# Expert rows weighted and gated on their way out of PSUM and added by DMA into a plane that starts as the residual

## The reference, cut to what matters

```python
x = x + g1 * mix                                        # the residual, x2 in the kernel
h = rms_norm(x, norm2_w) * (1.0 + sc2) + sh2
x = x + g2 * hier_moe(h, ...)
# hier_moe: each token takes the best of 4 groups, then the best two of its 8 experts (32 in all)
wts = p_grp * top_p / jnp.sum(top_p, axis=-1, keepdims=True)      # one weight for each of the two
hid = silu(h @ w_exp_gate[e]) * (h @ w_exp_up[e])                 # 1024 -> 256
y   = sum over the two experts of wts * (hid @ w_exp_down[e])     # 256 -> 1024
```

## Time and profile before

| | |
|---|---|
| median of three runs | 1171.54 us |
| the profiled execution's own time | 1173.27 us |
| its span, first to last instruction | 1171.5 us |
| busy: PE, DVE, ACT, POOL | 1029.5, 433.0, 311.7, 164.0 us |
| mean granted TensorE clock | 0.954 of full speed |
| moved by DMA over the span | 204.20 MB, 174 GB/s |

### The profile page before, as it was taken

One profiled execution on the slowest core, in us unless ns is written; L12 is line 12 of the kernel. 1 busy time (PEld: TensorE's weight loads), 2 busy tenths in 40 slices (PEclk: granted clock), 3 DMA queues, 4 the chain that ended last, 5 costly groups with the idle time before them and its releaser, 6 DMA issues.

```text
span 1171.5 us, 14600 instructions
## 1 busy us (share of the span) xinstructions
PE 1029.5 (88%) x5595; PEld 562.0 (48%) x5595; DVE 433.0 (37%) x845; ACT 311.7 (27%) x619; POOL 164.0 (14%) x257
## 2 busy tenths in 40 slices
PE   4999999999998889989999999999919997797870
PEld 2444456666554679988544444444513332232220
DVE  1433036787775864645501200224460111100116
ACT  4122144566652434324310000111211111111111
POOL 0100020011000327770300000000110121101110
PEclk9999999999999999999999999999959999988995
DMA  9821152436110111300371110142535999999956
GB/s 387 346 90 46 70 183 88 190 116 216 73 72 16 42 39 41 98 8 1 109 284 72 72 72 10 63 166 85 216 103 192 396 401 422 422 424 423 423 226 269
DMA packets 43644, 204.20 MB, mean 174 GB/s; under 512 B 16736, under 2 KB 22320, under 8 KB 31536
## 3 DMA queue, kind: packets, MB, share of 16 engines
q1 hardware_dynamic: 32576, 171.92, 37.3%
q0 software_dynamic: 10416, 30.45, 7.3%
q10 hardware_dynamic: 576, 0.82, 0.2%
HBM read 191.79 MB, written 19.76 MB: 181 GB/s over the span
## 4 chain that ended last, share of the span: by engine, by line
PE 75%; DVE 11%; issue 5%; DMA 5%; ACT 2%; POOL 2%; SPq 0%; POOLq 0%; DVEq 0%; ACTq 0%
PE bank L1717 25%; PE bank L2311 11%; PE bank L1839 7%; PE bank L2332 5%; PE bank L2156 3%; PE bank L2154 3%; PE bank L1681 2%; PE bank L1998 2%; PE bank L1888 2%; DMA arena<-in_w_up 2%; PE bank L2299 1%; PE bank L2008 1%; PE bank L1732 1%; DMA arena<-in_w_blocks 1%; PE bank L1824 1%
## 5 line engine op out<-in xcount | busy, mean ns | idle before, releaser
L1717 PE MATMUL bank<-arena 128*128 128x512 f32 x672 | 292.6, 591 | 0.0
L1717 PEld LDWEIGHTS bank<-arena 128*128 128x128 f32 x672 | 125.4, 189 | 151.8 <-issue 151.8
L2311 PE MATMUL bank<-arena 128*32 128x512 f32 x1152 | 140.5, 642 | 32.1 <-issue 30.8
L1839 PE MATMUL bank<-arena 128*128 128x320 f32 x384 | 120.0, 454 | 0.0
L2311 PEld LDWEIGHTS bank<-arena 128*32 128x32 f32 x1152 | 42.4, 117 | 117.9 <-issue 117.9
L1839 PEld LDWEIGHTS bank<-arena 128*128 128x128 f32 x384 | 69.7, 192 | 35.7 <-issue 11.2
L1649 DVE TENSOR_TENSOR arena<-arena,bank 128x256 f32<-128x256 f32 x18 | 7.6, 421 | 174.6 <-ACT arena L1104 174.6
L1493 DVE TENSOR_TENSOR arena<-arena,bank 128x512 f32<-128x512 f32 x10 | 6.9, 688 | 168.1 <-PE bank L2156 168.1
L2332 PE MATMUL bank<-arena 128*32 128x512 f32 x576 | 65.8, 595 | 1.0 <-DVE arena L1642 1.0
L1026 ACT ACTIVATE arena<-bank 128x512 f32<-128x512 f32 x20 | 12.0, 598 | 145.7 <-PE bank L1717 145.7
L1104 ACT ACTIVATE arena<-bank 128x256 f32<-128x256 f32 x18 | 6.9, 385 | 164.2 <-PE bank L2311 164.2
(11 more groups left out here) (315 smaller groups left out, 1387.7 us busy)
## 6 DMA issues: line engine op xcount, KB each, us to landing
arena<-in_w_up SPq DMA_DIRECT2D x32, 2048.0 KB, 18.1
arena<-in_w_blocks SPq DMA_DIRECT2D x27, 2048.0 KB, 8.0
arena<-in_w_down SPq DMA_DIRECT2D x32, 1024.0 KB, 21.9
arena<-y_scratch SPq DMA_DIRECT2D x10, 512.0 KB, 7.3
arena<-in_bias POOLq DMA_DIRECT2D x3, 1536.0 KB, 10.7
arena<-mod_scratch POOLq DMA_DIRECT2D x8, 512.0 KB, 10.9
arena<-in_x SPq DMA_DIRECT2D x5, 512.0 KB, 7.0
gram_scratch<-arena SPq DMA_DIRECT2D x10, 256.0 KB, 2.5
```

What stands on the lines that cost most here:

```text
L1717: last = mm(bank, hT[:, k, tok0[i]:tok0[i] + P], w[:, k, :], start=(k == 0), stop=(k == KC - 1))
L1839: last = mm(banks[5 + half][:, 0:HTOK], w[:, k, :], hT[:, k, half * HTOK:(half + 1) * HTOK], start=(k == 0), stop=(k == KC - 1))
L2311: last = mm(banks[2 + e % 2][at, :], rowsT[e % 2][:, k, at], eup[expert % SLOTS_W][:, k, :], start=(k == 0), stop=(k == KC - 1))
```

## The change

Weights and gate rows are put together per slot while the tiles run, the product leaves PSUM already weighted and gated, and the scatter adds it to a plane that was filled with x2. The plane is then copied to the output.

- `y_scratch` has 640 rows and 128 spare ones. SP fills it with x2 in six DMAs right after `up_in(3)`, before it waits for the route.
- The weight of a pair (fp32) is cut into three fp16 pieces, spread into `named_w`, and brought to the slots by ten more small matmuls at the head of PE's branch; five DVE instructions put the pieces together as `slot_w0` (context tokens) and `slot_w1` (latent ones).
- Per tile ACT makes context gate row x `slot_w0` (`gate_part`), DVE adds latent gate row x `slot_w1` (`gate_rest`), and both banks are multiplied with that by DVE (`out_rows`). ACT's copy of bank 6 is gone.
- An empty slot of partition p is sent to spare row 640 + p instead of being passed over. Each tile's scatter becomes two, one for each run of the tile's first expert and the rest (64 and 64 rows in twelve tiles, 96 and 32, 64 and 64 or 32 and 96 in the six wide ones), so that no token appears twice in one. Each adds to what stands in HBM, and each waits until the one before it has landed (`scattered`).
[...]
- The read-back, the weighting, gating and residual add at the end are gone. Five DMAs copy the plane from HBM to the output in HBM.

The diff, cut to its core (left out: semaphore names, places of the tables, and the branch that is not taken):

```diff
@@ -320,9 +324,14 @@
...
         rows_out = [flat(hT)[:, (2 + n) * D:(3 + n) * D] for n in range(3)]
-        slot_f = flat(merged)[:, 4 * D:4 * D + 2 * TILES]
-        empty = flat(merged)[:, 4 * D + 2 * TILES:4 * D + 4 * TILES]
-        slots = flat(merged)[:, 4 * D + 4 * TILES:4 * D + 6 * TILES].bitcast(I32).rearrange("p (n e) -> p n e", n=2)
+        per_tile = [flat(merged)[:, 4 * D + n * TILES:4 * D + (n + 1) * TILES] for n in range(14)]
+        slot_f, empty, slots, slots_to, slot_w0, slot_w1 = per_tile[:6]
+        slots, slots_to = slots.bitcast(I32), slots_to.bitcast(I32)
+        slot_p = flat(merged)[:, 4 * D + 6 * TILES:4 * D + 9 * TILES].rearrange("p (n e) -> p n e", n=3)
+        slots_moved = {64: per_tile[12].bitcast(I32), 96: per_tile[13][:, 0:6].bitcast(I32), 32: per_tile[13][:, 6:12].bitcast(I32)}
+        left = per_tile[9][:, 0:2 * T].unsqueeze(2)
+        pieces = flat(merged)[:, 4 * D + 10 * TILES:4 * D + 10 * TILES + 3 * T].bitcast(FP16).rearrange("p (a n) -> p a n", n=3)
+        gated = [x2[:, n, :] for n in range(2)]
...
+
+        def expert_rows(n):
+
+            first = next(at.start for at, q in tile_parts(n) if q != tile_parts(n)[0][1])
+            return slice(0, first), slice(first, P)
 
...
@@ -563,6 +568,9 @@
...
             up_in(3)
+            for i in range(T):
+                sp.dma_start(t["y_scratch"][i * P:(i + 1) * P, :], x2[:, i, :]).then_inc(S["y_base"], 16)
+            sp.dma_start(t["y_scratch"][TOK:TOK + P, :], x2[:, 0, :]).then_inc(S["y_base"], 16)
...
                     up_in(e)
...
+                for i in range(T):
+                    sp.wait_ge(S["y_ready"], i + 1)
+                    sp.dma_start(t["y"][i], x2[:, i, :]).then_inc(S["y_out"], 16)
             with sp.Else():
                 sp.wait_ge(S["route_ready"], 2)
+                for at, table in slots_moved.items():
+                    sp.dma_start(table[0:P - at, :], slots_to[at:P, 0:table.shape[1]]).then_inc(S["moved"], 16)
...
 
-                for n in range(3):
-                    sp.wait_ge(S[f"expert_out{n}"], 16 * len(range(n, TILES, 3)))
+                sp.wait_ge(S["scattered"], 32 * TILES)
                 for i in range(T):
-                    for r in range(2):
-                        sp.dma_start(y_part(i, r), t["y_scratch"][(r * T + i) * P:(r * T + i + 1) * P, :]).then_inc(y_loaded(i)[0], 16)
-            for i in range(T):
-                sp.wait_ge(S["y_ready"], i + 1)
-                sp.dma_start(t["y"][i], x2[:, i, :]).then_inc(S["y_out"], 16)
+                    sp.dma_start(t["y"][i], t["y_scratch"][i * P:(i + 1) * P, :]).then_inc(S["y_out"], 16)
...
@@ -731,21 +739,27 @@
...
-                pool.wait_ge(S["slots_ready"], 1)
+                pool.wait_ge(S["chosen"], 3)
+                pool.wait_ge(S["y_base"], 16 * (T + 1))
                 for e in range(TILES + 3):
+                    if e == 3:
+                        pool.wait_ge(S["moved"], 16 * 3)
                     if e < TILES:
                         if e >= 4:
                             pool.wait_ge(S["rowsT_mm"], 2 * (e - 3))
                         pool.indirect_dma_start(out=rows_in[e % 4], out_offset=None, in_=t["h_scratch"],
-                                                in_offset=bass.IndirectOffsetOnAxis(ap=slots[:, 0, e:e + 1], axis=0),
+                                                in_offset=bass.IndirectOffsetOnAxis(ap=slots[:, e:e + 1], axis=0),
                                                 bounds_check=TOK - 1, oob_is_err=False).then_inc(S[f"rows_in{e % 4}"], 16)
                     if e >= 3:
                         o = e - 3
                         pool.wait_ge(S["acc_done"], o + 1)
                         pool.wait_ge(S["s_out2"], o + 1)
-                        pool.indirect_dma_start(out=t["y_scratch"], out_offset=bass.IndirectOffsetOnAxis(ap=slots[:, 1, o:o + 1], axis=0),
-                                                in_=rows_out[o % 3], in_offset=None,
-                                                bounds_check=2 * TOK - 1, oob_is_err=False).then_inc(S[f"expert_out{o % 3}"], 16)
+                        for n, at in enumerate(expert_rows(o)):
+                            if o or n:
+                                pool.wait_ge(S["scattered"], 16 * (2 * o + n))
+                            pool.indirect_dma_start(out=t["y_scratch"], out_offset=bass.IndirectOffsetOnAxis(ap=(slots_moved[at.start] if n else slots_to)[0:at.stop - at.start, o:o + 1], axis=0),
+                                                    in_=rows_out[o % 3][at, :], in_offset=None, bounds_check=TOK + P - 1, oob_is_err=True,
+                                                    compute_op=ALU.add).then_inc(S["scattered"], 16)
...
@@ -1090,11 +1105,13 @@
...
-                def out_rows(e):
-                    act.wait_ge(S["down_mm"], e + 1)
-                    if e >= 3:
-                        act.wait_ge(S[f"expert_out{e % 3}"], 16 * (e // 3))
-                    step(sc.activation(rows_out[e % 3][:, 0:HALF], banks[6][:, :], ACT.Copy), "acc_done")
+                def gate_part(e):
+                    if e == 0:
+                        act.wait_ge(S["slot_w"], 1)
+                        act.wait_ge(S["y_base"], 16 * (T + 1))
+                    if e >= 2:
+                        act.wait_ge(S["s_out2"], e - 1)
+                    step(sc.activation(gated[e % 2], gate2_bc[:, 0, :], ACT.Copy, scale=slot_w0[:, e:e + 1]), "gated")
 
                 rowsT_out(0)
                 for e in range(TILES):
@@ -1104,17 +1121,9 @@
                     step(sc.activation(sg[:, e % 2, 0:D_FF], banks[2 + e % 2][:, 0:D_FF], ACT.Silu), "silu_done")
                     if e + 1 < TILES:
                         rowsT_out(e + 1)
-                    if 1 <= e < TILES - 1:
-                        out_rows(e - 1)
                     act.wait_ge(S["hidT_mm"], e + 1)
                     step(sc.activation(hidT[:, e % 2, 0:2 * P], banks[4 + e % 2][:, 0:2 * P], ACT.Copy), "hidT_ready")
-                out_rows(TILES - 2)
-                out_rows(TILES - 1)
-                act.wait_ge(S["weights_ready"], 1)
-                for i in range(T):
-                    act.wait_ge(*y_loaded(i))
-                    a = y_part(i, 0)
-                    step(sc.activation(a, a, ACT.Copy, scale=wts[:, 1, i, :]), "weighted")
+                    gate_part(e)
...
@@ -1569,31 +1578,39 @@
...
-            for n in range(2):
-                step(v.tensor_tensor(named[:, :, n, :], reached[:, :, 0:TILES], payload[:, :, n:n + 1].to_broadcast([P, 2 * T, TILES]), ALU.mult),
-                     "dest_ready" if n else "dve_step")
+            step(v.tensor_tensor(named, reached[:, :, 0:TILES], payload[:, :, 0:1].to_broadcast([P, 2 * T, TILES]), ALU.mult), "chosen")
...
             dve.wait_ge(S["logit_mm"], 6)
-            table = banks[0][:, 256:256 + 2 * TILES]
+            table = banks[0][:, 256:256 + TILES]
             step(v.tensor_scalar(empty, table, 0.0, float(NOWHERE), ALU.is_equal, ALU.mult))
             step(v.scalar_tensor_tensor(slot_f, table, -1.0, empty, ALU.add, ALU.add))
-            step(v.tensor_copy(slots, slot_f.rearrange("p (n e) -> p n e", n=2)), "slots_ready")
+            step(v.tensor_copy(slots, slot_f), "chosen")
             barrier(dve, 3)
+            dve.wait_ge(S["router_exp"], 1)
+            step(v.tensor_reduce(wts[:, 0], ex[:, 1, :, 0:4], AX_X, ALU.add))
+            step(v.scalar_tensor_tensor(wts[:, 0], ex[:, 1, :, 4:5], 1.0, wts[:, 0], ALU.add, ALU.mult))
+            step(v.reciprocal(wts[:, 1], wts[:, 0]))
+            step(v.tensor_tensor(wts[:, 2], wts[:, 1], ex[:, 1, :, 4:5], ALU.mult))
+            weight = wts[:, 1:3].rearrange("p r t n -> p (r t) n")
+            step(v.tensor_copy(pieces[:, :, 0:1], weight))
+            step(v.tensor_tensor(left, weight, pieces[:, :, 0:1], ALU.subtract))
+            step(v.tensor_scalar(pieces[:, :, 1:2], left, float(PIECE), None, ALU.mult))
+            step(v.scalar_tensor_tensor(left, pieces[:, :, 1:2], -1.0 / PIECE, left, ALU.mult, ALU.add))
+            step(v.tensor_scalar(pieces[:, :, 2:3], left, float(PIECE * PIECE), None, ALU.mult))
+            step(v.tensor_tensor(named_w, reached[:, :, 0:TILES].unsqueeze(2).to_broadcast([P, 2 * T, 3, TILES]),
+                                 pieces.unsqueeze(3).to_broadcast([P, 2 * T, 3, TILES]), ALU.mult), "chosen")
+            step(v.tensor_scalar(slot_f, slot_f, payload[:, 0, 1:2], None, ALU.min))
+            step(v.tensor_copy(slots_to, slot_f))
             one = [1, N_RANKED, N_RANKED]
...
             step(v.tensor_reduce(order_f[0:1].unsqueeze(2), holds, AX_X, ALU.add))
             step(v.tensor_copy(order[0:1], order_f[0:1]), "route_ready")
-            dve.wait_ge(S["router_exp"], 1)
-            step(v.tensor_reduce(wts[:, 0], ex[:, 1, :, 0:4], AX_X, ALU.add))
-            step(v.scalar_tensor_tensor(wts[:, 0], ex[:, 1, :, 4:5], 1.0, wts[:, 0], ALU.add, ALU.mult))
```

(44 more changed lines are left out.)

35 lines of the change are left out of this document (17 added, 18 removed).

## The result

The changed kernel takes 1231.87 us, the median of five runs (1220.24 to 1236.13), the kernel before 1172.03 (five runs, 1170.84 to 1175.04). The ratio is 1.0493, 95% interval 1.0467 to 1.0518: 5% slower. 1195 was predicted, 1162 to 1228 the range. The direction was right; the size was not, and the measured median lies 4 us above the range.

What follows compares the result with a forecast made beforehand. From tile 9 PE waits for weights on full DMA engines. First scatter at 902.2, eight pairs at 15, eight at 19.1, 12.2 for the last two, then 0.2 and a 7.8 copy gave 1195.2 us; range 1162 to 1228.

Steps and rivals of the forecast that it cites:

- Forecast A: Tile stage: the chain of scatters paces the tiles, 1195 us, own range 1183 to 1215, chance 0.42.
- The signs named for it: Trace: paired scatters waiting on scatters, up matmuls 18 us apart or more from tile 9, DMA share below 0.98.
- B: DMA engines: chain hides behind weights, only bytes cost; with the adding's read paid 1176 to 1187 us, chance 0.18.
- C: DMA engines, 900 to 1122 us: adding costs only its writes, 9.4 us against 15.5 gained; 1165 us, chance 0.20.
- E: Whole kernel: gain and bytes cancel within 2.3 us, or the end isn't shorter; 1173 us, chance 0.05.
- eight early pairs: First eight tiles' scatter pairs: 15 us each, between PE's own pace of 12.0 and 19.1 where engines are full.
- eight pairs under load: Next eight tiles, engines full: 19.1 us per scatter pair, two landings of 9.4 us with 0.3 us of issue.
- last two pairs: Tiles 16 and 17, emptying queues: 6.1 us per scatter pair, two landings of 2.9 us and 0.3.
- hand-over and copy: After the last scatter: 0.2 us, then 7.8 us for copying 2.62 MB HBM to HBM.
- with 0.3 us of issue: Price of a tile's two chained scatters: 0.3 us of issue besides two landings, 19.1 us where engines are full.
- D: Tile stage: adding slower than thought, 19.1 us a tile or more from the first tile; 1228 up to 1240, chance 0.15.
- The end: After the last tiles: copy replaces read-back and DVE work, 15.5 us gained, 7.6 at the least, if load is gone.

Runs made afterwards that it cites:

- e4: Kernel before with each tile's scatter in two halves, each waiting for the last landing; plain writes, live rows only, old end: 1195.57 us.
- e9: Kernel before with each scatter in two plain halves and no wait between them, live rows only, old end: 1174.37 us.
- e10: e3 with a wait for the previous landing before each whole-tile adding scatter: 1175.67 us.
- e3: Changed kernel with one whole adding scatter per tile, no waits between scatters, each pair in its own row, empty slots passed over: 1173.16 us.
- e7: Kernel before plus the six DMAs filling the plane with the residual, and the waits for them: 1172.59 us.
- e8: Changed kernel's weighting and gating out of PSUM, but one plain unchained scatter per tile, no filling, read-back and DVE adds at the end: 1168.53 us.
- e1: Changed kernel with scatters writing instead of adding; split, chain of waits and spare rows stay: 1189.44 us.
- e2: Changed kernel with empty slots passed over instead of added to spare rows; adding, split and chain stay: 1207.12 us.
- e6: Changed kernel with POOL issuing each gather ahead of the scatter of the tile five places before, not three: 1219.88 us.

## Why the prediction was right and wrong

**The bound was read rightly.** Forecast A, that the chain of scatters paces the tiles, is what the trace shows, and e4, e9 and e10 show it to be the cause. The signs named for it came: pairs whose waits end with the scatter before, up matmuls further apart (19.5 us on average from tile 9 on, 16.4 before), a DMA share below 0.98 from tile 9 on (0.97, from 1012 to 1161 us), a lower granted clock that is not on the path, DVE work gone from the end. The share is a weak sign, though: it was 0.98 from 900 to 1012 us, where the chain already set the pace. One did not come: the time after the last matmul was to be 17.5 us and is 34. B and C are out, as they had the chain hidden. What they would have been was run for the live rows only: e3 comes to 1173.2, what the change adds to its stage cost 15 us, and the end gave them back, which is the balance that E had described.

**What I priced at nothing cost nothing:** the filling (e7), the work on the engines per tile (e8: last scatter 0.7 us later than before), the tables (first scatter 1.7 us earlier than before). The split and its index columns, which had no term, cost nothing either (e9, plain).

**The sum, term by term**, against the profiled span of 1218.4 (predicted 1195.2, so 23.2 to find):

| term | predicted | measured | difference |
|---|---|---|---|
| first scatter | 902.2 | 900.5 | -1.7 |
| eight early pairs | 8 x 15 = 120 | 140.7 (17.6 each) | +20.7 |
| eight pairs under load | 8 x 19.1 = 152.8 | 144.7 | -8.1 |
| last two pairs | 2 x 6.1 = 12.2 | 21.0 | +8.8 |
| hand-over and copy | 8.0 | 11.5 | +3.5 |

**The step that failed** is "with 0.3 us of issue" in the price of a pair. The start of the next scatter comes 0.8 us after the landing that it waits for, after the first half and after the second, so a pair has 1.6 us of it and not 0.3. If every pair of the sum is read as two landings and 0.3 us, as its terms for load and for empty queues are built, the miss falls apart like this:

| | predicted | measured | difference |
|---|---|---|---|
| first scatter | 902.2 | 900.5 | -1.7 |
| 36 landings | 279.6 | 278.0 | -1.6 |
| between them | 18 x 0.3 = 5.4 | 35 x 0.81 = 28.4 | +23.0 |
| hand-over and copy | 8.0 | 11.5 | +3.5 |

The gap could have been read before: DVE's last copy ends at 1138.61 + 0.69 = 1139.30 and the scatter that it releases starts at 1140.14, 0.84 us later.

That the landings sum to what was predicted is luck, for their errors cancel. The early pair of 15 us leaves 7.4 us for a landing, and it was 8.0 on average; the loaded one took 9.4, and it was 9.2 over tiles 8 to 12 but 8.2 over the eight tiles that the sum counts; the last four took 2.9, and it was 4.7.

**The early pair** of 15 us was put between PE's 12.0 and the full load's 19.1 on the thought that emptier queues would bring the landing down. It measured 17.6, and half of the difference is the gap. The queues were not empty: the DMA share is 0.99 from 900 to 1041 us, and it was 0.99 in the same place before, where the whole scatters of the first eight tiles took nearly as long as the later ones:

```profile
L746 POOL DMA_INDIRECT y_scratch<-arena x8: 1004/1016/1027, 902.2 to 987.7; - x8
...
DMA to landing us min/median/max: 6.9/9.6/11.8
```

D had the loaded pair from the first tile on, 1228; it came nearer than A, and I had given it 0.15. But D's 19.1 is more than the early 17.6, and its end is as short as A's, so its time is near in part because two errors cancel.

**The end.** Its landings were priced with the plain 2.9 us; that an adding half takes 4.7 was in no row, but I had added something for the read under load and nothing here. The copy took 11.5 us instead of 7.8. From the start of the last multiply to the end it is 33.9 us, as long as the old end (32.9); the gain of 15.5 us that the sum counted was lost to four landings in a row. Without the chain it is there: 15.7 us in e3.

**The loaded pair** (19.1 predicted; 20.1 over tiles 8 to 13, less in the last ones) was right in size. Its landing of 9.4 us under full load was right too (9.2), but partly for a wrong reason, as the number of live rows hardly counts: over tiles 8 to 12 halves of 64 and of some 35 written rows both take 7.9 us (e1, e4). The adding counts, 9.2 us for 64 rows. On empty queues halves take 3.2 (64 written), 4.7 (64 added) and 2.5 us (35 written).

**What stays open.** The median lies 11.6 us above the profiled execution, so that much of the miss can't be read in a trace. The changed kernel spreads 16 us over five runs and e1_plain 11 over four, but e2, e4 and e6, which are chained too, only 5 over four each, so the chain alone does not explain the spread. Why landings under load differ so little with their rows (7.9 us for 35 as for 64) no run tells.

## What to carry to other kernels

A wait for a DMA's landing costs what a landing costs under the load of its stage, not on empty queues: here 8 to 11 us instead of 3 to 5, and 0.8 us more until the next one starts. One such wait per tile hid behind a tile of 12 to 17 us; two, from splitting the same rows, set the pace, with plain writes in the tiles of 12 to 13 us and with adding in all of them. So compare the chain with the shortest tile, not with the mean one. Before a read-modify-write is used to save work on engines that stand idle, give each contribution a place of its own, keep the plain write, and move to the idle engines only the arithmetic: that part alone was worth 0.2% here (0.4% with the read-back on two queues, which is not told apart).

## What the runs showed of the hardware that was not expected

- Under load the time from issue to landing of an indirect DMA grows far less than its rows. Over tiles 8 to 12 (medians) half scatters took 7.9 us with 35 and with 64 written rows, 8.6 with 35 added and 9.2 with 64 added ones; whole plain ones of 71 rows took 10.9, whole adding ones 11.3 (e3) and 11.4 (e10). Two halves in a row are dearer than one whole.
- A scatter that waits for a landing, or for DVE, starts 0.8 us after it: median 0.81 over the 35 gaps of the changed kernel, 0.86 behind DVE's copies in the kernel before.
- An adding scatter keeps the DMA engines busy 5.4 us per MB, a plain one 2.6. The Trainium skill (DMA: Bandwidth & Descriptors, Rules for kernel authors) says that an accumulate reads its destination and writes it later; the doubled time agrees with that. Its fixed 2 us plus bytes over 436 GB/s (same page, Anatomy of one DMA) gives an estimated 2.6 us for half a tile; the runs show 3.2 us plain and 4.7 us adding on empty queues, 7.9 and 9.2 us under load, and the measurement decides.
- POOL takes longer to issue an adding scatter: 1.44 us for a half where the plain half took 0.91, 1.59 us for a whole tile where the plain one took 1.02.
- A copy of 2.62 MB from HBM to HBM took 11.5 us from the first issue to the end, 228 GB/s, while the read-back moved 5.24 MB in 15.7 us.
